# A routed-experts kernel: the second expert's first two weight transfers asked for earlier, the first tiles' rows asked for by another engine

## What is computed

```python
def moe(x, w_router, router_bias, w_gate, w_up, w_down):
    t = x.reshape(B * S, D)
    combine = route(t, w_router, router_bias).astype(x.dtype)
    h = jax.nn.silu(jnp.einsum('td,edf->tef', t, w_gate)) * jnp.einsum('td,edf->tef', t, w_up)
    y = jnp.einsum('tef,efd->td', h * combine[:, :, None], w_down)
    return y.reshape(B, S, D)

xp = layer_norm(ALPHA * xp + mix_p, ln1_g[i], ln1_b[i])
xp = layer_norm(ALPHA * xp + moe(xp, ...), ln2_g[i], ln2_b[i])
```

## Time and profile before

| | |
|---|---|
| three runs | 1110.19, 1109.82, 1109.48 us; median 1109.82 |
| the profiled execution | 1110.86 us; its span, first to last instruction, 1109.2 us |
| TensorE busy | 1039.2 us (94%), granted clock 0.975 of full speed |
| VectorE, ScalarE, GpSimd busy | 377.2, 195.8, 94.9 us |
| bytes moved | 297.24 MB, 268 GB/s over the span |

### The profile page before, as it was taken

The page is one execution under the profiler, slowest core; times in us unless marked ns, Lnnn a source line. Parts: engine busy times, 40 slices in busy tenths (PEclk is TensorE's granted clock), DMA queues, the critical chain, the costliest instruction groups (busy, mean ns, idle before and its releaser), DMA issues.

```text
span 1109.2 us, 36492 instructions
## 1 busy us (share of the span) xinstructions
PE 1039.2 (94%) x16051; PEld 878.1 (79%) x16051; DVE 377.2 (34%) x858; ACT 195.8 (18%) x444; POOL 94.9 (9%) x179
## 2 busy tenths in 40 slices
PE   7989999989999798999999999998899999999995
PEld 6767777744566398999999997675699999999982
DVE  1334444423366532121221212976112212212127
ACT  1234444430043121000000001111200000100010
POOL 0011121241000200000000002101100000000012
PEclk9999999989999889999999999988899999999999
DMA  9512342714205899999999997861599999999935
GB/s 337 196 56 90 121 145 90 256 35 135 88 14 215 333 360 331 361 374 397 375 383 374 388 389 240 312 276 66 188 368 399 385 394 371 379 393 384 401 102 218
DMA packets 80479, 297.24 MB, mean 268 GB/s; under 512 B 10216, under 2 KB 40304, under 8 KB 72095
## 3 DMA queue, kind: packets, MB, share of 16 engines
q1 hardware_dynamic: 54327, 248.91, 60.6%
q10 hardware_dynamic: 17952, 25.24, 6.8%
q0 software_dynamic: 8144, 22.29, 5.7%
HBM read 255.91 MB, written 40.97 MB: 268 GB/s over the span
## 4 chain that ended last, share of the span: by engine, by line
PE 81%; DVE 8%; DMA 4%; issue 3%; POOL 2%; ACT 1%; SPq 0%; ACTq 0%; POOLq 0%; DVEq 0%
PE PS L1000 16%; PE PS L1023 16%; PE PS L1012 15%; PE PS L895 5%; PE PS L648 4%; PE PS L695 3%; PE PS L985 3%; PE PS L711 3%; PE PS L603 2%; PE PS L704 2%; PE PS L625 2%; POOL expert_rows L1178 1%; PE PS L668 1%; PE PS L798 1%; PE PS L685 1%
## 5 line engine op out<-in xcount | busy, mean ns | idle before, releaser
L1000 PE MATMUL PS<-arena,ring 128*64 128x96 f32 (+1 forms) x4096 | 186.7, 250 | 8.0 <-DVE arena L1907 8.0
L1000 PEld LDWEIGHTS PS<-arena,ring 128*64 128x64 f32 x4096 | 177.0, 139 | 14.7 <-issue 14.7
L1023 PE MATMUL PS<-arena,ring 128*64 128x96 f32 (+1 forms) x4096 | 178.3, 248 | 10.1 <-DVE arena L1943 5.4
L1023 PEld LDWEIGHTS PS<-arena,ring 128*64 128x64 f32 x4096 | 173.8, 138 | 12.0 <-DVE arena L1943 6.5
L1012 PE MATMUL PS<-arena,ring 128*64 128x96 f32 (+1 forms) x4096 | 175.8, 246 | 0.7 <-issue 0.6
L1012 PEld LDWEIGHTS PS<-arena,ring 128*64 128x64 f32 x4096 | 171.9, 137 | 1.1 <-issue 1.1
L1907 DVE STREAM_TRANSPOSE arena<-arena 128x768 uint32<-128x768 uint32 x34 | 54.3, 1597 | 138.2 <-ACT arena L1384 124.0
L1951 DVE COPY arena<-PS 128x384 f32<-128x384 f32 x32 | 17.8, 557 | 160.9 <-PE PS L1023 160.9
L1395 ACT ACTIVATE arena<-PS 128x384 f32<-128x384 f32 x32 | 15.7, 490 | 252.8 <-PE PS L1023 252.8
L895 PE MATMUL PS<-ring,arena 128*128 128x512 f32 x128 | 57.2, 607 | 0.7 <-issue 0.7
L576 PE MATMUL PS<-C 128*128 128x256 f32 (+1 forms) x160 | 52.2, 483 | 0.2 <-issue 0.2
(11 more groups left out here) (300 smaller groups left out, 1113.1 us busy)
## 6 DMA issues: line engine op xcount, KB each, us to landing
ring<-w_up SPq DMA_DIRECT2D x32, 2048.0 KB, 18.1
ring<-w_down SPq DMA_DIRECT2D x32, 2048.0 KB, 20.9
ring<-w_gate SPq DMA_DIRECT2D x32, 2048.0 KB, 17.7
expert_out<-arena ACTq DMA_DIRECT2D x32, 384.0 KB, 13.9
arena<-expert_rows ACTq DMA_DIRECT2D x128, 96.0 KB, 9.5
expert_rows<-ring SPq DMA_DIRECT2D x6, 1920.0 KB, 9.9
ring<-cache_ckv SPq DMA_DIRECT2D x56, 128.0 KB, 2.2
expert_out<-ring SPq DMA_DIRECT2D x1, 4608.0 KB, 25.3
```

The source lines that it names most:

```text
L1000: last = nc.tensor.matmul(bank(s, KF, n)[at:at + 64, f, :], wg[w][:, k, P * f + at:P * f + at + 64], x[:, k, :], start=(k == 0), stop=(k = ...
L1023: last = nc.tensor.matmul(bank(4 + m // 4, 4, n)[at:at + 64, m % 4, :], wd[w][:, f, P * m + at:P * m + at + 64], hh[:, f, :], start=(f == ...
```

## The change

SyncE no longer waits for `scat` and no longer asks for the rows of tiles 0 and 1; the wait for `mix_ps` with expert 1's gate and up weights (two transfers of 2 MB into buffer 0) stands directly behind expert 0's gate weights. The wait for `scat` and the eight row transfers are now ScalarE's, between `take_rows(0, 4)` and the exponential of the sample router. Nothing else is touched; line numbers below the first place are smaller by three, below the second equal again.

```diff
--- before.py
+++ after.py
@@ -512,9 +512,6 @@
                     first_weights(wd, "w_down", 0, 1, q["wd_ld"])
                     sp.wait_ge(pv_ps, 5)
                     first_weights(wg, "w_gate", 0, 1, q["wg_ld"])
-                    sp.wait_ge(scat, 128)
-                    load_rows(sp, 0, 0, slice(0, CAP))
-                    load_rows(sp, 0, 1, slice(CAP, 2 * CAP))
                     sp.wait_ge(mix_ps, NT)
                     first_weights(wg, "w_gate", 1, 0, q["wg_ld"])
                     first_weights(wu, "w_up", 1, 0, q["wu_ld"])
@@ -1451,6 +1448,9 @@
             samples()
             deviation(0, 0, 4)
             take_rows(0, 4)
+            act.wait_ge(scat, 128)
+            load_rows(act, 0, 0, slice(0, CAP))
+            load_rows(act, 0, 1, slice(CAP, 2 * CAP))
             experts(0)
 
             for step in range(2 * NT + 1):
```

## The result

Over twenty runs of each, the median went from 1108.92 to 1116.63 us: the change costs **7.7 us**, ratio 1.0073 with a 95% interval of 1.0054 to 1.0092, that is 6.0 to 10.2 us. The forecast was 8.8, from 1109.82. Single runs of one and the same kernel lie over 10 us apart (1103.08 to 1113.74 for before), so one profiled execution says little about the sum and much about each place.

The account below looks back on a forecast made before the run. TensorE's chain bounds the kernel, its expert stage waiting on scatters, rows and transposition, not on the moved weights. Terms 8.9 - 0.1 + 0 + 0 = +8.8 us on 1109.8 give 1118.6 us, range 1116.5 to 1122.0.

Parts of the forecast that it names:

- The path: Into the expert stage: scatters landed 383.50, rows asked and landed +3.88, transposed +1.65, tile 0's first matmul 389.03 us.
- SyncE's ask: Expert 1's gate and up weights, released by `mix_ps`, asked at 377.65 and 378.1 instead of 387.19 and 387.67 us.
- The scatters' end: Before the rows' ask: scatters alternate packet by packet with the early weights, landing at 392.4 instead of 383.50, +8.9 us.
- the stragglers: Last scatter packets after the bulk: 2.3 us might hide or come again after 391.3; the middle, 392.4, was taken.
- ScalarE's ask: Row transfers asked by ScalarE instead of SyncE: 3.78 against 3.88 us to the transposition, -0.1 us.
- The other price: ScalarE free for the rows' ask only at 385.8: +2.3 us if scatters landed at 383.50, otherwise in their shadow.
- Exponential and sample router: Behind ScalarE's new wait: exponential and sample selection come later but stay hidden behind tile 0's 8.7 us of gate matmuls.
- The clock: TensorE's clock at tile 0's start: low level 0.50 as before, taken as 0, bounds -0.9 and +0.9 us.
- Rival A: Scatters get half the bytes beside the weights; rows then meet the remaining weights: +5.1, 1114.9 us; chance 0.18.
- Rival A's argument from 292 to 91 packets: In the expert stage, 454 to 458 us, 1 KB rows get more than one packet per weight packet.
- Rivals B and D: B: scatters unharmed, ScalarE asks rows at 385.8, at least +2.3, 1112.1 us, chance 0.09. D: late `mix_ps` nullifies change; excluded.
- Rival C: Expert stage limited by transfers: early weights remove 7.2 us of TensorE's stops, giving 1104.9 us; chance 0.03.

Follow-up runs that it names:

- The 4 KB packets: The full change with each of the two early weight transfers split into four, in packets of 4 KB; ratio 1.0069 to the kernel before.
- half the weights: The full change, but expert 1's up weights are asked only when the scatters have landed; ratio 1.0094 to the kernel before.
- the rows by ScalarE alone: The full change, but SyncE waits for the scatters before asking for expert 1's gate and up weights; ratio 1.0113 to the kernel before.

## Why the prediction was right

- **The path** was read rightly: scatters, rows, transposition, tile 0. The early weights had no waiting user; tile 1 started 20.5 us after tile 0 with the change, 21.0 in the earlier trace rows.
- **SyncE's ask** was off by 5.2 us: 372.46, not 377.65. The step that failed took VectorE's 377.57 for the time at which `mix_ps` reached its count in every execution; the other traces have 371 to 375. Luck made up for most of it: the weights' first packets were taken to come 1.0 us after their ask and came some 3.5 us after it, near 376, where 378.6 was forecast. As the working said, the last byte doesn't hang on either, for the engines are busy throughout: bulk until 391, as forecast. But the two streams did not run out together, as the working had it; the weights were nearly through at 388 and the scatters had 1.07 MB to go alone.
- **The scatters' end**, +8.9: they were awaited at 393.40 (+9.9). The turns, packet by packet, are shown by three pairs of queues (224 to 230, 216 to 215, 452 to 461) and by the size of the packets; that the scatters come last is what the turns decide, and when the last byte leaves is given by all the bytes together. The term that was 1.0 us short is the stragglers: I halved their 2.3 us, and they came again in full (391 to 393.40).
- **ScalarE's ask**, -0.1 and in the shadow of the scatters: 3.89 us against 3.88, and alone it costs nothing (ratio 0.9996). The other price, +2.3 for ScalarE not being free before 385.8, hung on the same 377.57: it was free at 381.2, and in both runs with undisturbed scatters it asked for the rows as they landed.
- **Exponential and sample router** behind ScalarE's wait: hidden, the gate's matmuls end 8.8 us after tile 0's start, 8.7 in the earlier trace rows.
- **The clock**, 0: 0.50 for the first 5 us of tile 0, as before.
- **Rival A** was priced too low. If the scatters get half, the rows come into the weights' packets, and I let them end "not much later than the weights", +5.1. The 4 KB packets came out at +9.0, half the weights at +11.1 and the rows by ScalarE alone at +11.8 for tile 0, because the many small row packets move mostly after the weights have gone, at 190 GB/s (0.38 MB from 396 to 398 in the run of the rows by ScalarE alone). So the sign of the result hung on no share at all, which I had not seen: **each order of these transfers that puts the 4 MB ahead of or beside the rows costs about the same.**
- **Rival A's argument from 292 to 91 packets** The earlier trace rows doesn't hold either. Expert weights are asked one matrix at a time there, and the four us contain a gap between two of them. The transfers by queue in before, from 455.5 to 456.5 us and from 458 to 458.5 us, when the next matrix flows:

```profile
q10 hardware_dynamic: 89, 0.08, 46.2%
q1 hardware_dynamic: 9, 0.05, 25.3%
...
q1 hardware_dynamic: 29, 0.11, 78.4%
q10 hardware_dynamic: 29, 0.02, 21.5%
```

- **Rivals B and D** are contradicted: the scatters were harmed (+9.9), and the ask moved by 14.7 us.
- **Rival C** (a lead of the transfers) is contradicted: tile 0 came 9.9 us later, more than the 7.2 it allows, the transfer engines stood idle for tile 0's first 9 us, and 4.7 us of stops remained, as many as in one trace of before.
- **The sum** was 8.8 and the median moved by 7.7; tile 0 by 9.9. That the median came within 1.1 us of the forecast is partly luck: the stragglers made tile 0 about 1 us later than the sum has it, and some 2 us less than tile 0's delay reached the median, which is within its interval (6.0 to 10.2) and not explained.

## What to carry to other kernels

An early ask is only free if nothing that someone waits for shares the transfer engines: list what is in flight at the new place, and count **packets**, not bytes, on both sides. A stream of small packets (scattered rows, gathered rows) beside a stream of large ones gets its share of turns, not of bytes, and ends when the large one does or later. The last byte of both leaves when all their bytes are through at the engines' rate, whatever the turns; the turns only decide which stream is done early. Keep the small, urgent one ahead of the large one in the same queue, as this kernel did before. And count a place's times from an event just ahead of it in the same trace: that repeated to 0.1 us in three traces of before, where the whole run varies by 10.

## What the runs showed of the hardware that was not expected

- Two queues whose packets flow at once shared the engines one packet for one, at each pair of sizes and kinds seen here: software against hardware (224 to 230), hardware against hardware (216 to 215), 4 KB against 4 KB (452 to 461). Counts over a stretch in which one queue has a gap, as the 292 to 91 of the earlier trace rows, say nothing of the share.
- Weights asked while the scatters had the engines full hardly flowed for some 3.5 us (3 packets against 284), where the first packets in the earlier trace rows came after 1.0 us.
- Rows in pieces of 1 KB move at 190 GB/s with the engines to themselves (99% share), less than half the 416 of large packets.
- The Trainium skill, "DMA: Bandwidth & Descriptors", section "Queues, rings and completion order", has an engine drain a whole packet of typically 9 to 17 descriptors before it turns to the next queue. What the trace records as packets, each of one row or one 16 KB piece, comes out evenly from both queues over some us (452 to 461, all 4 KB or less). Turns of 9 to 17 on either side would give even counts too, so the runs show the equal share and not how long a turn is.
- One kernel's first expert stage took 285 to 293 us in three executions, with the steps ahead of it, counted from the first scatter's ask, the same to 0.1 us.
